# A mixture-of-experts tail: expert results in pairs, added by indirect transfers to the residual in DRAM, in place of padded stores and a final gather

## What is computed

```python
g_prob = softmax(ht @ wg + bg);   p_g, g_idx = top_k(g_prob, 1)          # 8 groups
e_sel  = logits of the 8 experts of that group
top_l, top_i = top_k(e_sel, 2);   gate_w = p_g * softmax(top_l)          # 2 experts per token
expert = g_idx * 8 + top_i                                              # both of one group
y[token, c] = (silu(x @ w_gate[e]) * (x @ w_up[e])) @ w_down[e]          # 1024 -> 512 -> 1024
x = x + sum_c gate_w[token, c] * y[token, c]
out = rmsnorm(x, final_norm_g)
```

## Time and profile before

| | |
|---|---|
| median of 3 runs | 2502.29 us |
| the profiled execution's own time | 2498.37 us |
| its span, first to last instruction | 2496.6 us |
| TensorE busy | 2239.4 us, 90% of the span |
| DMA busy share | 0.9 or more in the slices from 1560 us on |
| mean granted clock of TensorE | 0.966 |

### The profile page before, as it was taken

One profiled execution on the slowest core, in us unless ns is written; L12 is line 12 of the kernel. 1 busy time (PEld: TensorE's weight loads), 2 busy tenths in 40 slices (PEclk: granted clock), 3 DMA queues, 4 the chain that ended last, 5 costly groups with the idle time before them and its releaser, 6 DMA issues. The chain is left out here.

```text
span 2496.6 us, 31843 instructions
## 1 busy us (share of the span) xinstructions
PE 2239.4 (90%) x13520; PEld 1635.2 (65%) x13520; DVE 790.2 (32%) x1619; ACT 476.0 (19%) x839; POOL 228.5 (9%) x209
## 2 busy tenths in 40 slices
PE   8899978999999997989987989988888899898884
PEld 5788867888887676878873456555555555555552
DVE  6453156243324777353261231111111111111102
ACT  3222214231132544232211030000000000000001
POOL 0720000011000000830000010000000000000001
PEclk9999989999999999999998989999999999999997
DMA  9533112254330002434163539999999999999996
GB/s 279 176 118 132 51 46 102 95 172 135 120 102 18 14 22 71 141 127 156 38 145 134 182 131 381 425 426 426 426 426 427 426 426 426 427 426 427 426 425 265
DMA packets 135058, 581.43 MB, mean 233 GB/s; under 512 B 27682, under 2 KB 41622, under 8 KB 101078
## 3 DMA queue, kind: packets, MB, share of 16 engines
q1 hardware_dynamic: 117843, 419.67, 44.4%
q0 software_dynamic: 15920, 155.50, 15.3%
q10 hardware_dynamic: 1152, 4.19, 0.5%
HBM read 541.50 MB, written 37.63 MB: 232 GB/s over the span
## 5 line engine op out<-in xcount | busy, mean ns | idle before, releaser
L468 PE MATMUL ps<-w_parts,u_parts 128*128 128x512 f32 (+3 forms) x2016 | 425.6, 372 | 13.5 <-DVE u_parts L648 6.8
L2744 PE MATMUL ps<-mem,mem_u 128*64 128x256 f32 x2880 | 351.4, 399 | 73.6 <-DMA mem<-in_expert_w_up 67.6
L468 PEld LDWEIGHTS ps<-w_parts,u_parts 128*128 128x128 f32 x2016 | 362.7, 189 | 71.7 <-DVE u_parts L648 8.0
L2744 PEld LDWEIGHTS ps<-mem,mem_u 128*64 128x64 f32 x2880 | 227.5, 143 | 201.4 <-issue 109.5
L435 DVE TENSOR_TENSOR w_parts<-w_raw,w_parts 128x2048 fp32r<-128x2048 f32 (+3 forms) x76 | 172.4, 2270 | 391.3 <-ACT w_parts L430 391.3
L2829 DVE TENSOR_TENSOR mem_c<-mem_c,ps 128x256 f32<-128x256 f32 x64 | 27.0, 421 | 742.6 <-issue 648.2
L430 ACT CAST w_parts<-w_raw 128x2048 fp32r<-128x2048 f32 (+3 forms) x76 | 135.0, 1776 | 485.4 <-PE ps L468 193.7
L466 PE MATMUL ps<-u_parts,w_parts 128*128 128x512 f32 x768 | 176.8, 390 | 0.0
L1444 PE MATMUL ps<-w_parts,u_parts 128*128 128x512 f32 x768 | 175.8, 391 | 0.0
L2744 PE MATMUL ps<-mem_u 128*64 128x256 f32 x1216 | 147.7, 398 | 28.2 <-DMA mem_u<-in_expert_w_up 25.2
L2757 PE MATMUL ps<-mem,mem_c 128*64 128x512 f32 x736 | 166.0, 593 | 2.8 <-DMA mem<-in_expert_w_down 2.3
(11 more groups left out here) (377 smaller groups left out, 2254.3 us busy)
## 6 DMA issues: line engine op xcount, KB each, us to landing
mem<-in_expert_w_down SPq DMA_DIRECT2D x46, 2048.0 KB, 35.1
mem<-in_expert_w_up SPq DMA_DIRECT2D x45, 2048.0 KB, 36.1
mem<-in_expert_w_gate POOLq DMA_DIRECT2D x43, 2048.0 KB, 14.2
mem_u<-in_expert_w_up SPq DMA_DIRECT2D x19, 2048.0 KB, 35.5
mem_u<-in_expert_w_down SPq DMA_DIRECT2D x18, 2048.0 KB, 35.6
mem_u<-in_expert_w_gate POOLq DMA_DIRECT2D x18, 2048.0 KB, 14.2
w_raw<-in_od_w_in SPq DMA_DIRECT2D x18, 1024.0 KB, 5.1
ypad<-mem_u SPq DMA_DIRECT2D x128, 128.0 KB, 30.8
```

Of the source, the lines that this page charges most:

```text
L468: mm = pe.matmul(out, u[:, x, ku, g.t * P:(g.t + 1) * P], w[y][:, kk, :], start=first, stop=last)
L2744: mm = pe.matmul(ps[SLOTS * h:SLOTS * (h + 1), bank, 0:256], x[:, kk, :], w[:, kk, 256 * h:256 * (h + 1)], start=kk == 0, stop=kk == KD - 1)
```

## The change

1. The experts are done in another order (`expert_at`): positions 2p and 2p+1 are experts of different groups, so that no token is in both. The parts of a pair come in the order gate, up, gate, up, down, down (`part_at`, `load_expert_part`).
2. `result` is called once per pair. Its matmuls put one expert's 64 slots on partitions 0 to 63 and the other's on 64 to 127, with columns 0 to 511 in one bank and 512 to 1023 in the next: 128 whole rows of 4 KB.
3. ScalarE copies the two banks with a scale per partition, the gate's weight of the slot (`k.slot_w`). This weight and the slot's row number (`k.slot_row`) come from 8 small matmuls per four experts (`place`, bank 7) of the `picks` with a table (`Route.table`) and three small VectorE operations (`settle`). `Route.places` goes. An unused slot gets row number 1023.
4. GpSimd adds the 128 rows to `k.sum_dram` (512 x 1024) by one indirect transfer with `compute_op=add`; rows beyond 511 are out of bounds and no error. There are 32 such transfers. They replace the 128 stores of SyncE. A buffer is used again two pairs later, when its transfer has landed.
5. `k.sum_dram` is filled in `mix_out` with the residual (one 2 MB store). That frees `H0`, which becomes an eighth home. Eight parts are loaded before `moe`. GpSimd's queue now issues two loads (gate and up of a pair's first expert) after each pair's result, then the pair's add; SyncE's the other four of each six parts.
6. `Finish` waits for all adds and loads 4 x 512 KB of `k.sum_dram` by SyncE, with no gather, weight or add; square, root, scale and store are as before. The load of the gains is moved ahead.
7. `mem_in` no longer writes zeros.

```diff
+def expert_at(i):
+    q, s = divmod(i, FOUR)
+    j, half = divmod(q, 2)
+    return EPG * (FOUR * half + s) + j
...
-HOMES = (U0, U0 + SLOT, RING + SLOT, RING + 2 * SLOT, RING, Y0, Y0 + SLOT)
+HOMES = (U0, U0 + SLOT, RING + SLOT, RING + 2 * SLOT, RING, Y0, Y0 + SLOT, H0)
...
+            sp.wait_ge(added, 2 * NT)
+            sp.dma_start(k.sum_dram.rearrange("(m p) n -> p m n", p=P), h).then_inc(k.sum_set, 16)
...
         def _(pool):
-            for n in range(N_HOMES, 3 * NE):
-                e, i = divmod(n - N_HOMES, 3)
-                if i == 2:
+            pool.wait_ge(k.sum_set, 16)
+            for e in range(n_pairs):
+                n = N_HOMES + 6 * e + 4
+                if n < n_parts:
                     pool.wait_ge(y_done, e + 1)
                     load_expert_part(k, pool, n)
-            for i in range(STORES):
-                pool.wait_ge(stored[i], 32 * (NE // STORES))
+                    load_expert_part(k, pool, n + 1)
+                pool.wait_ge(rows_ready, 2 * e + 2)
+                pool.indirect_dma_start(k.sum_dram, bass.IndirectOffsetOnAxis(ap=k.slot_row[:, e:e + 1].bitcast(U32), axis=0),
+                                        yn[:, e % STORES, :], None, bounds_check=S - 1, oob_is_err=False,
+                                        compute_op=ALU.add).then_inc(added[e % STORES], 16)
             last.gpsimd(pool)
...
+            def place(q):
+                if q == 0:
+                    pe.wait_ge(table_set, 1)
+                else:
+                    pe.wait_ge(placed, q)
+                for i in range(2):
+                    for m in range(NT):
+                        mm = pe.matmul(ps[:, PLACE, 4 * i:4 * i + 4], picks[:, q % 2, m, P * i:P * (i + 1)],
+                                       pairs(k.slot_table[:, :, m, expert_at(FOUR * q)]), start=m == 0, stop=m == NT - 1)
+                mm.then_inc(place_mm, 1)
...
-                if e:
-                    result(e - 1)
+                if e and e % 2 == 0:
+                    result(e // 2 - 1)
...
         for m in range(NT):
-            for c in range(2):
-                pool.indirect_dma_start(self.rows[c][:, m, :], None, k.ypad,
-                                        bass.IndirectOffsetOnAxis(ap=k.dest[:, c, m:m + 1].bitcast(U32), axis=0)
-                                        ).then_inc(self.gathered[2 * m + c], 16)
...
+        for s in self.more.moe_added:
+            sp.wait_ge(s, 16 * (NE // 2 // STORES))
+        sp.wait_ge(self.more_done, 1)
+        x = k.sum_dram.rearrange("(m p) n -> p m n", p=P)
+        for m in range(NT):
+            sp.dma_start(self.x3[:, m, :], x[:, m, :]).then_inc(self.loaded[m], 16)
```

More of the change, by code:

```diff
@@ L135, in spread, with pairs @@
     return bass.AP(ap.tensor, ap.offset, dims)
+def pairs(ap):
+    step = ap.ap[-1][0]
+    return bass.AP(ap.tensor, ap.offset, [list(ap.ap[0]), [step, 2], [step, 2]])
 def backwards(ap):
@@ L2635, in blocks, with table @@
         k.link(dve, dve.tensor_copy(k.flag.bitcast(I32), self.tmp64[:, NE - 1:NE]))
[L2637 to L2656, removed]
+    def table(self, dve):
+        k, OH = self.k, self.OH
+        for c in range(2):
+            self.tt(dve, OH[c], OH[c], spread(k.gate_w[:, c, :], 2, NE), ALU.mult)
+        self.tt(dve, OH[0], OH[0], OH[1], ALU.add)
+        k.link(dve, dve.tensor_reduce(self.token_w, OH[0].rearrange("p m (g j) -> p m j g", g=EG), AX_X, ALU.add))
+        lo, hi = (k.slot_table[:, i, :, :].rearrange("p m (g j) -> p m g j", g=EG) for i in range(2))
+        k.link(dve, dve.tensor_copy(hi, spread(self.token_w, 2, EG)))
+        self.tt(dve, lo, spread(self.token_w, 2, EG), hi.bitcast(F32), ALU.subtract)
+        k.link(dve, dve.tensor_copy(k.slot_table[:, 2, :, :], spread(k.row_code, 2, NE)))
 def since(eng, sem, v):
@@ L2787, in _, with rows @@
         def _(act):
-            def rows(e):
-                act.wait_ge(y_done, e + 1)
-                if e >= STORES:
-                    act.wait_ge(stored[e % STORES], 32 * (e // STORES))
-                act.copy(yn[:, e % STORES, :], ps[:, ROWS + e % 2, :]).then_inc(rows_ready, 1)
+            def rows(pair):
+                act.wait_ge(y_done, pair + 1)
+                if pair % 2 == 0:
+                    act.wait_ge(placed, pair // 2 + 1)
+                if pair >= STORES:
+                    act.wait_ge(added[pair % STORES], 16 * (pair // STORES))
+                for c in range(2):
+                    act.activation(yn[:, pair % STORES, 512 * c:512 * (c + 1)], ps[:, ROWS + c, :], ACT.Copy,
+                                   scale=k.slot_w[:, pair:pair + 1]).then_inc(rows_ready, 1)
             for e in range(NE):
@@ L2798, in _ @@
                 act.activation(sg[:, e % 2, :], ps[:, GATE, 0:256], ACT.Silu).then_inc(silu_done, 1)
-                if e:
-                    rows(e - 1)
-            rows(NE - 1)
+                if e and e % 2 == 0:
+                    rows(e // 2 - 1)
+            rows(n_pairs - 1)
             last.scalar(act)
@@ L2823, in _ @@
                 take(piece)
+            k.route.weights(dve)
+            k.route.table(dve)
+            dve.sem_inc(table_set, 1)
             for e in range(NE):
@@ L2958, in step @@
                     for part in range(2):
[L2959 to L2960 removed]
+                        pe.matmul(ps[:, 0, SLOTS * kk:SLOTS * (kk + 1)], k.hn_parts[:, part, m, kk, :],
+                                  self.pick[:, m, :], start=m + part == 0, stop=m == NT - 1 and part == 1)
+            for m in range(NT):
+                mm = pe.matmul(ps[0:SLOTS, 7, 0:4], self.pick[:, m, :], pairs(self.place[:, :, m]), start=m == 0, stop=m == NT - 1)
             mm.then_inc(self.x_done, 1)
@@ L3073, in vector @@
         for m in range(NT):
-            for c in range(2):
-                dve.wait_ge(self.gathered[2 * m + c], 16)
-                if c:
-                    dve.wait_ge(self.summed, 2 * m + 1)
-                dve.scalar_tensor_tensor(out=x3[:, m, :], in0=self.rows[c][:, m, :], scalar=k.gate_w[:, c, m:m + 1],
-                                         in1=x3[:, m, :], op0=ALU.mult, op1=ALU.add).then_inc(self.summed, 1)
-            if m:
-                scale(m - 1)
-        scale(NT - 1)
+            scale(m)
 def program(nc, dram, out, stop=None):
```

218 lines of the change are left out of this document (121 added, 97 removed).

## The result

| | median | range | runs | ratio to before |
|---|---|---|---|---|
| before | 2502.09 us | 2500.09 to 2502.56 | 5 | |
| changed kernel | 2491.36 us | 2485.59 to 2493.55 | 5 | 0.9953, 95% interval 0.9938 to 0.9968 |
| changed kernel, run again with experiments 5 to 8 | 2489.77 us | 2486.77 to 2494.88 | 6 | 0.9959 (0.9947 to 0.9971) |

The change saves 10 to 11 us, which is clear of the noise. 30.8 were forecast, 2472 us. The profiled execution took 2491.36 us too, and its span is 2489.5.

The account below looks back on a forecast made before the run. The mixture was taken to be bound by DMA bytes. Stores -38.7, eighth home -4.9, adds +24.7 and tail -11.9 sum to -30.8 us, forecasting 2472 us, range 2455 to 2503.

Parts of the forecast that it names:

- stores gone: Mixture's stream: SyncE's 126 stores go, 16.5 MB at 426 GB/s, all real traffic, 38.7 us less.
- eighth home: Start of the mixture: the eighth part passes in a gap where DMA engines were idle, 4.9 us less in the stream.
- adds: Mixture's stream: 1024 rows pass twice, 8.4 MB at the gathers' 340 GB/s, 24.7 us more (bounds 9.8 and 37.0).
- tail: From the stream's end to the span's end: 28.7 us against 40.6, so 11.9 us less.
- A few engines carry the adds: Rival, stream: low slots load few DMA engines, the fullest sets the pace; adds cost 51.7 us, total 2499 us; chance 0.24.
- six tenths of it full, so T = 2456: Kernel before: the stream's end, read from 255 GB/s in the window 2450 to 2460 us, leaving a 40.6 us tail.
- the second is tight: GpSimd's queue: a first expert's up part, needed after some 29 us, lands in 28; TensorE waits, the stream loses nothing.
- The store of the residual: Before the mixture: its 4.9 us fit the idle half of the window 1465 to 1476 us, costing nothing.
- Unused slots move too: Rival, stream: out-of-bounds rows are still fetched, 4096 rows pass instead of 1024, 98.8 us, total 2546 us; chance 0.15.
- The stream starves: Rival, stream: DMA engines idle while homes are held and parts come late; up to 2491 us; chance 0.08.
- the written bytes: Sign, DRAM: near 4.2 MB written for the adds; some 17 MB written or read would show that unused slots move.
- a mean share below 1 in the stream: Sign for few engines carrying the adds: mean DMA busy share below 1 while TensorE still waits for loads.

Follow-up runs that it names:

- experiments 5 to 8: Four runs measured beside one another: the changed kernel alone, two edits of it, and one edit of the kernel before, whose median there was 2499.78 us.
- experiment 8: Kernel before without the stores of the first 63 experts, its final gathers reading other DRAM rows of the same size: 2467.09 us, ratio 0.9861.
- experiment 7: Changed kernel with its eighth part loaded only after the first gate projection is done: 2491.08 us, ratio 0.9965.
- experiment 5: The changed kernel itself, unedited, measured again as the control: 2489.77 us, ratio 0.9959.
- experiment 4: Changed kernel with all row numbers out of bounds, so the 32 transfers stay but no row is added: 2458.88 us, ratio 0.9839.
- experiments 1 and 2: Changed kernel with used rows on other partitions: spread over the engines (fullest 80 rows), 2471.25 us; crowded on two engines (fullest 247 rows), 2523.21 us.

## Why the prediction was off, step by step

| term | forecast | the runs |
|---|---|---|
| stores gone | -38.7 | -32.7 (experiment 8 against before) |
| eighth home | -4.9 | -1.3, within the noise (experiment 7 against 5) |
| adds | +24.7 | +30.9 (experiment 5 against 4) |
| tail | -11.9 | -6.6 (35.2 to 28.6 in the profiles) |
| sum | -30.8 | -9.7; measured -10.0 to -10.7 |

Each number of the last column is uncertain by some us (the stores' by -31 to -38), so that the last line closes so well is luck. What the table shows is that all four terms missed to the same side, by 3.6 to 6.2 us, the adds and the stores most.

**Adds.** "Two passes at the gathers' pace" was right in the passes and wrong in the division: "with the work even over the engines" did not hold. Two passes were a fair mean price (327 ns a row, 64 rows on a mean engine: 21 us), and spread over the engines they let the kernel take 2470 to 2471 us. That this is within 2 us of the forecast of 2472 is luck: the spread adds cost 12.4 us instead of 24.7, and the other three terms brought some 15 us less than forecast. The stream went at the pace of the fullest engine, the rival *A few engines carry the adds*, to which I gave 0.24. Its mechanism is shown by experiments 1 and 2, in both directions; its own price, 24.7 x 2.1 = 51.7, was too high by 21 us. The better product was rows by price of a row, 134 x 0.327 = 43.8, less a slack of 13 us that is measured and not explained.

**Stores.** Here "38.7 us less" was bytes by rate, with nothing said of what comes next. The stores in the stream are 126 x 64 = 8064 packets, and 8064 x 84 ns / 16 = 42 us of each engine, so the traffic was not sized too high. What failed was the step from traffic to time, "they were all of it real traffic". Why some 4 to 6 us of it did not show stays open. The two things seen at the end of experiment 8, landing marks in two halves (8 up to 2423.55, 8 from 2428.98 on) and 20.7 us of TensorE's own work, stand in the kernel before as well and so explain no difference; and the upper end of the interval, 38 us, is nearly the forecast.

**Eighth home.** The part did pass in the gap, at no cost, and 3.4 of its 4.9 us were lost right behind, where the DMA engines have a share of 0.97 in place of 1.01. As I read it, a part that lands ahead brings the stream forward only as far as releases of homes come forward too, and those go by TensorE.

**Tail.** The tail after the change was forecast to 0.1 us (28.7, measured 28.6), which is closer than its parts deserve. Up to the issue of the four loads the pieces held (14.0 and 14.0 us). Behind it, 8.4 us of loads and 3.0 for the last tile were put in; in the chain the first load takes 3.8 us, and then ScalarE does the four tiles one behind the other, 1.6 us each, and ends behind the last landing. The two sums are 11.4 and 11.5. The control's tail is 29.8. The tail before was not forecast so well: "six tenths of it full, so T = 2456" turned a mean share into an end, as if all engines stopped at once. The last part landed at 2461.4, so the old tail was 35.2 us and not 40.6. The same window's 0.65 could have told me of the ragged end.

**What held.** TensorE's extra work stayed hidden: it had 80 us of 800 free, and the 128 small matmuls took 16.9 us of the 24 allowed. The load of GpSimd's up parts, "the second is tight", made no wait: no up part is in the list. An add took GpSimd 1.64 us where 1.0 was put in, which no one waits for. The store of the residual cost nothing that can be seen, but not for the reason given: it was issued at 1470.1 and landed 14.4 us later, at 1484.5, not within the window from 1465 to 1476 (share 0.47 there, where 0.49 was). It ran into the gap behind it, and the three loads issued from 1481.1 on still landed by 1499.4, ahead of the first projection at 1503.2. *Unused slots move too* is excluded by the packets of 8 bytes, *The stream starves* by a share of 1.01 in the 800 us; only the first 40 us of the stream had less (0.97). The starving stream's 2491 us were met all the same, by another cause. **Signs that misled:** the written bytes (experiment 4); and for few engines I had named "a mean share below 1 in the stream"; the mean stayed at 1.01 in the changed kernel, and showed the skew only at the end.

## What to carry to other kernels

When transfers use only some of the partitions, count their bytes for each DMA engine and not on average: a stream that is spread evenly over all engines waits for the fullest one, and here another order of slots, at no cost, was worth 19 us, more than the whole change had brought. The mean busy share did not show this skew while eight parts were in line; look for it in the last windows and in the landing marks of the last load, and compare with a kernel that has no skew, since here even that one ended at half the share for 8 us. Read the end of a stream from the last landing and not from a mean share, and see in the chain whether a transfer or an engine came last there.

## What was not expected of the hardware

An added row that is out of bounds leaves a packet of 8 bytes and 9 ns, 2764 of them in the packets counted above, and no other cost that could be seen; an added row takes 327 ns where a written one takes 160. HBM bytes on the page are declared, not moved (35.80 MB with 1024 rows and with none). Ahead of all this TensorE's first long matmuls vary from one execution to another. Timeline of TensorE from 0 to 40 us, changed kernel, then the one before:

```profile
14.12 7.00 PE L834 MATMUL ps<-mem 33*12 33x512 f32 x8
```

```profile
14.06 3.96 PE L835 MATMUL ps<-mem 33*12 33x512 f32 x8
```

The same eight matmuls took 4.14 us in the control, the same kernel as the first, where the mixture's first projections began 2.9 us earlier too (1500.2 and 1503.2 us). In experiment 8, an edit of the kernel before, they took 7.00. So it is no part of the change, and a difference of 3 us between two single executions of this program is not one of the kernels. What makes them slow isn't shown: the granted clock is 1.00 from 14 to 18 us in both executions above.
